# Three 64-wide transposes of a chunked recurrence made as 128x128 transposes, with the sorting of heads left to the copies

## The chip, the cores and the metric

The kernel runs on one core of a Trainium2 chip. The metric is the device time of one execution in microseconds. TensorE multiplies matrices into PSUM, ScalarE and VectorE read PSUM and SBUF, GpSimd works on SBUF alone, and SyncE issues the transfers. Each engine works through its own queue in order and waits for others at semaphores.

## The reference

The program is three small models in a row, each with two layers on 512 positions of width 1024, in float32. The change lies in the last layer of the third model, in a recurrence that runs forwards and backwards over the sequence for 16 heads of width 64. For each head and direction:

```python
def wkv7_step(state, inp):
    r, w, k, v, a, b = inp
    sa = jnp.einsum('...ij,...j->...i', state, a)
    state = (state * w[..., None, :] + sa[..., :, None] * b[..., None, :]
             + v[..., :, None] * k[..., None, :])
    y = jnp.einsum('...ij,...j->...i', state, r)
    return state, y

def rwkv7_bidir_branch(p, mu, w0, w2, a0, a2, k_k, k_a, r_k, lnx_g, lnx_b):
    ...
    init = jnp.zeros((2, bsz, C_HEADS, C_HEAD_DIM, C_HEAD_DIM), jnp.float32)
    xs = (to_scan(r), to_scan(decay), to_scan(k), to_scan(v), to_scan(-kk), to_scan(kk * a))
    _, y = lax.scan(wkv7_step, init, xs)
    y = jnp.moveaxis(y, 0, 2)
    y_sum = y[0] + jnp.flip(y[1], axis=1)
    ...
```

## The kernel before, in words

The function `wkv` does this recurrence in chunks of 64 positions. Its work is cut into 16 steps, one for each pair of heads (c, 0 to 7) and direction (d, 0 or 1). The even steps (d = 0) go forwards, the odd ones (d = 1) backwards. Steps 0 and 1 and steps 14 and 15 are written out; steps 2 to 13 are three rounds of a loop with four steps in it.

An array such as VQ (the values) or BK (the two scaled factors, bhat in `BK[:, 0]` and khat in `BK[:, 1]`) has 128 partitions and 512 columns. Its partitions are channels: 0 to 63 are those of the first head of the pair, 64 to 127 those of the second. Its columns are positions, eight chunks of 64. Some products contract over positions, and for them the step needs the arrays VT, BT and KT, in which the positions of a chunk stand on the partitions: head 0 on partitions 0 to 63, head 1 on 64 to 127, and in the free dimension chunk j with 64 channels.

Each step does two things at once, in an order of instructions written out by hand in `step` for each engine. It prepares its own chunks (projection of the next raw data, norms, decays, the three transposes, three groups of products, five levels of a triangular inverse). And it runs the serial chain over the eight chunks of the step before, of which every link is a few small products on TensorE (`ch_g`, `ch_sa`, `ch_ys`), with a small copy on VectorE (`gk`, L3798), one on ScalarE (`san`, L3720) and the state's update on VectorE (`upd`, L3805) between them. These links stand among the preparation, so that neither waits for long.

The places that matter here, in the order of TensorE's queue in one step:

- `ch_sa(1)`, then the transpose of the values (mark "tv") and that of bhat ("tb"). Each is 16 products of 64x64 through `heads` (L3527): eight chunks times two heads, with the data as the stationary operand and the 64x64 identity as the moving one. They write PSUM banks 4 and 1.
- The product "bon" with the whole array (L3632), and `ch_ys(1)`.
- The transpose of khat ("tk", again 16 products), into bank 4. It waits until ScalarE has copied the values out of this bank ("vt") and VectorE has made khat (L3866).
- `ch_g(2)`, which waits for the state's update `upd(1)`.
- "sa", 16 products, which wait for the copy "bt" on ScalarE and for rhat on VectorE (L3867).
- "srb", 16 products of 64x128 into banks 4 and 5, which wait for the copy "kt" on ScalarE. Behind srb stand `ch_sa(2)`, another 16 such products and the levels.

ScalarE's queue at this place: the copy of a projection, `san(1)` (L3720), then the three copies of whole PSUM banks, "vt", "bt" and "kt" (L3775, one instruction of 128x512 each), then "as" (L3777), which waits for sa. VectorE's: rhat (L3867), "bo" (L3870 or L3872, behind TensorE's bon), `upd(1)` (L3805).

Of the kernel before, what the change touches and what calls it, by code (L numbers as in the profile page):

```python
# [10 lines left out]
ACT = mybir.ActivationFunctionType  # L11
# [4 lines left out]
P = 128  # L16
# [3381 lines left out]
def wkv(K, base, WDA, W2, RZ, out):  # L3398
# [7 lines left out]
    def room(n):  # L3406
        nonlocal at
        at += n
        return K.big(at - n, n)
# [8 lines left out]
    BK = room(2 * T).rearrange("p (m t) -> p m t", m=2)  # L3418
# [3 lines left out]
    RQ, KQ, VQ, LW, AA, L, EP, EN, RN, TMP = (room(T) for _ in range(10))  # L3422
# [6 lines left out]
    hr = lambda h: slice(64 * h, 64 * h + 64)  # L3429
# [3 lines left out]
    def halves(b):  # L3433

        two = K.psflat[:, b * 512:b * 512 + 1024].rearrange("p (b n) -> p b n", b=2)[:, :, 0:256]
        return two.rearrange("p b (j t) -> p b j t", t=64)
    block_of = lambda b, j: halves(b)[:, j // 4, j % 4, :]
    couple = lambda b: K.psflat[:, b * 512:b * 512 + 1024].rearrange("p (j m t) -> p j m t", m=2, t=64)
    chunks_of = lambda half: range(4) if half == "a" else range(4, 8)
    in_half = lambda a, half: a[:, 0:4, :] if half == "a" else a[:, 4:8, :]  # L3440
    bank_half = lambda b, half: halves(b)[:, "ab".index(half), :, :]
    levels = range(1, 6)
# [3 lines left out]
    AM = Marks(K, "wkv_act", "sw aa sqk ln rn ep en eplus ee vt bt kt as " + " ".join(f"t{l}a t{l}b" for l in levels))  # L3446
# [26 lines left out]
    with nc.Block() as block:  # L3473
# [38 lines left out]
        def _(pe):  # L3512
            same, one = K.c("same64"), K.c("cident")
# [10 lines left out]
            def heads(dst, lhsT, rhs, start=True, stop=True):  # L3524

                for h in range(2):
                    mm = pe.matmul(dst[hr(h)], lhsT[hr(h)], rhs[hr(h)], start=start, stop=stop, skip_group_check=True)  # L3527
                return mm
# [53 lines left out]
            def step(n, d, c, par, p, pd, nth, fin=None):  # L3582
# [34 lines left out]
                if n is not None:  # L3617
                    pe.wait_ge(DM.sem, DM.count(n, "max"))
                    K.apart(pe)
                    for j in range(8):  # L3620
                        mm = heads(K.ps[:, 4, 64 * j:64 * j + 64], VQ[:, 64 * j:64 * j + 64], one)
                    mm.then_inc(PM.step("tv"), 1)
                    pe.wait_ge(AM.sem, AM.count(n, "aa"))
                    pe.wait_ge(DM.sem, DM.count(n, "bhat"))
                    K.apart(pe)
                    for j in range(8):
                        mm = heads(K.ps[:, 1, 64 * j:64 * j + 64], BK[:, 0, 64 * j:64 * j + 64], one)
                    mm.then_inc(PM.step("tb"), 1)
                    pe.wait_ge(DM.sem, DM.count(n, "rk"))
                    if fin is not None:  # L3630
                        pe.wait_ge(K.sem("fin_act"), K.count("fin_act", 3 * fin[0] + 2))
                    pe.matmul(K.ps[:, 5, :], same, LW, start=True, stop=True).then_inc(PM.step("bon"), 1)  # L3632
                ch_ys(p, pd, 1)
                if n is not None:
                    pe.wait_ge(AM.sem, AM.count(n, "vt"))
                    pe.wait_ge(DM.sem, DM.count(n, "khat"))
                    K.apart(pe)
                    for j in range(8):
                        mm = heads(K.ps[:, 4, 64 * j:64 * j + 64], BK[:, 1, 64 * j:64 * j + 64], one)
                    mm.then_inc(PM.step("tk"), 1)  # L3640
                ch_g(p, pd, 2)
                if n is not None:
# [3 lines left out]
                    for j in range(8):  # L3646
                        mm = heads(block_of(0, j), AR[:, d, j, 0, :], BK[:, 0, 64 * j:64 * j + 64])
# [4 lines left out]
                    for j in range(8):  # L3652
                        mm = heads(couple(4)[:, j, :, :].rearrange("p m t -> p (m t)"), BK[:, 0, 64 * j:64 * j + 64],
                                   AR[:, d, j, :, :].rearrange("p m t -> p (m t)"))
                    mm.then_inc(PM.step("srb"), 1)
                ch_sa(p, pd, 2)
                if n is not None:
# [3 lines left out]
                    for j in range(8):  # L3661
                        mm = heads(couple(2)[:, j, :, :].rearrange("p m t -> p (m t)"), BK[:, 1, 64 * j:64 * j + 64],
                                   AR[:, d, j, :, :].rearrange("p m t -> p (m t)"))
                    mm.then_inc(PM.step("sk"), 1)
                ch_ys(p, pd, 2)
                for l in levels:
                    if n is not None:
                        pe.wait_ge(GM.sem, GM.count(n, f"c{l}"))
                        for half in "ab":
                            pe.wait_ge(DM.sem, DM.count(n, f"xt{l - 1}{half}" if l > 1 else "x0"))  # L3670
                            K.apart(pe)
                            for j in chunks_of(half):
                                mm = heads(block_of(0, j), C[:, j, :], XT[:, j, :])
                            mm.then_inc(PM.step(f"t{l}{half}"), 1)
                    ch_g(p, pd, l + 2)
                    if n is not None:
# [4 lines left out]
                        for half in "ab":  # L3681
                            pe.wait_ge(AM.sem, AM.count(n, f"t{l}{half}"))
                            K.apart(pe)
                            for j in chunks_of(half):
                                mm = heads(block_of(4, j), X[:, j, :], T1[:, j, :])
                            mm.then_inc(PM.step(f"ct{l}{half}"), 1)
                    ch_sa(p, pd, l + 2)
                    if n is not None and l < 5:
# [3 lines left out]
                        for half in "ab":  # L3692
                            for j in chunks_of(half):
                                mm = heads(block_of(2, j), T1[:, j, :], X[:, j, :])
# [5 lines left out]
            for m in range(4):  # L3700
                pe.wait_ge(K.sem("raw_kept"), K.count("raw_kept", m - 1))
                project(0, m)
            rounds(pe, step, finish)

        @block.scalar
        def _(act):
# [26 lines left out]
            def step(n, d, c, par, p, pd, nth, fin=None):  # L3733
# [38 lines left out]
                if n is not None:  # L3772
                    for name, src, dst, bank in (("vt", "tv", VT, 4), ("bt", "tb", BT, 1), ("kt", "tk", KT, 4)):
                        act.wait_ge(PM.sem, PM.count(n, src))
                        act.activation(dst[:, d].rearrange("p j t -> p (j t)"), K.ps[:, bank, :], ACT.Copy).then_inc(AM.step(name), 1)  # L3775
                    act.wait_ge(PM.sem, PM.count(n, "sa"))
                    act.activation(AS.rearrange("p (b j) t -> p b j t", b=2), halves(0), ACT.Copy).then_inc(AM.step("as"), 1)  # L3777
                san(p, pd, 2)
# [8 lines left out]
            for m in range(4):  # L3787
                keep(0, 0, m)
            rounds(act, step, finish)

        @block.vector
# [137 lines left out]
def rwkv_layer(K):  # L3929

    K.open(0, 4 * T)
    YD = K.big(0, 4 * T)
    K.open(4 * T, 9 * T)
    WD, WDA, W2, RZ = K.big(4 * T, T), K.big(5 * T, 2 * T), K.big(7 * T, 4 * T), K.big(11 * T, 2 * T)
    K.open(13 * T, 16 * T)
    FD = K.big(13 * T, 4 * T)
    DFT = K.big(17 * T, 8 * T).rearrange("p (i n) -> p i n", i=TT)
    DD = K.big(25 * T, 2 * P)
    four = lambda at, n: K.big(at, 4 * n).rearrange("p (g n) -> p g n", g=4)
    WF, WC = four(25 * T + 2 * P, P), four(25 * T + 6 * P, 2 * P)  # L3940
    with Parts(K, 8) as (hi, lo):
        rwkv_front(K, hi, lo, YD, FD, WD, WDA,
                   [(W2, "w2a2"), (RZ, "resets64"), (DFT, "dft"), (DD, "dft_d"), (WF, "fnet_w")])
    K.open(29 * T, 8 * T)
    fourier(K, FD, YD, DFT, DD, WF, WC, four(29 * T, 2 * T))
    K.shut()
    K.shut()
    K.open(13 * T, 43 * T)
    wkv(K, 13 * T, WDA, W2, RZ, K.X.rearrange("p k t -> p (k t)"))
    K.X, K.H = K.H, K.X  # L3950
    K.shut()
    K.shut()
    with Parts(K, 12) as (hi, lo):
        linear_deep(K, hi, lo, 6, add_to(K.X), feed=Feed(K, features(K.H) + tiles_of(YD, 4), hi, lo))
    K.shut()
# [144 lines left out]
```

## Time and profile before

| What | us |
|---|---|
| median of 3 runs | 4751.49 |
| lowest and highest | 4750.6, 4759.0 |
| the profiled execution, its own time | 4748.9 |
| its span | 4746.7 |
| TensorE busy (PE) | 4400.7, 93% of the span |
| VectorE busy (DVE) | 2457.6, 52% |
| ScalarE busy (ACT) | 1608.9, 34% |
| GpSimd busy (POOL) | 320.5, 7% |

The profile comes from one execution. Its span runs from the first to the last instruction; the 2.2 us between span and time lie around it. The `wkv` stage takes about 820 of the 4746.7 us, from 3824 to 4645, together with what directly follows its last step.

In the timelines below, neighbouring instructions of the same kind are merged into one row: its length is that of the whole group, and x is how many records are in it. A float32 product has two records on TensorE, a transpose in TensorE's own transpose form has one; "L3527 x64" is therefore 32 products. A matmul's record is longer than its pitch in the pipeline: the pitch is read from where the next group starts. What stands in brackets is the time in which the engine was idle before, and who released it.

### The profile page before, as it was taken

Reading aid. Unit: us, or ns where it says so; the run is one execution under the profiler, and the core shown is the slowest. Engines: PE = TensorE matmul, PEld = TensorE weight load, DVE = VectorE, ACT = ScalarE, POOL = GpSimd, SP = SyncE. Lnnn points to the kernel's source line nnn. Section 1 sums busy time; section 2 is a strip of 40 time slices with the busy share of each in tenths; the row PEclk is TensorE's granted clock in tenths of the full one; section 3 lists DMA queues with packets and bytes.
Section 4 is the critical chain, followed back from the end, with each engine's and each line's share of the span. In section 5 each row is a group of like instructions: output and inputs, shape, how many; then the busy total and the mean of one; then the engine's idle time right before and its main releaser. Section 6 shows DMA issues by size and latency. Waiting matters only on the chain. (4 is left out here: it accounts for less than half of the span.)

```text
span 4746.7 us, 79005 instructions
## 1 busy us (share of the span) xinstructions
PE 4400.7 (93%) x32172; PEld 3338.7 (70%) x32172; DVE 2457.6 (52%) x3963; ACT 1608.9 (34%) x2467; POOL 320.5 (7%) x307
## 2 busy tenths in 40 slices
PE   8898999899999989999998899978998999999987
PEld 7665788676688767888887644456877567766775
DVE  3634543433445331777777379943534355555553
ACT  2324322323322232666665210133222233334332
POOL 0120000000000000111111000000000022221220
PEclk9888999998999999999999999989998999999998
DMA  3201222221122232111111312111221210000101
GB/s 146 108 19 71 89 89 107 76 89 71 57 104 89 110 129 82 56 59 51 59 54 35 142 53 89 71 54 71 107 98 71 105 37 20 21 20 20 56 3 54
DMA packets 36644, 337.23 MB, mean 71 GB/s; under 512 B 4080, under 2 KB 6384, under 8 KB 18544
## 3 DMA queue, kind: packets, MB, share of 16 engines
q1 hardware_dynamic: 36336, 332.76, 19.0%
q8 instruction: 238, 3.90, 0.3%
q14 instruction: 70, 0.57, 0.0%
HBM read 320.16 MB, written 12.58 MB: 70 GB/s over the span
## 5 line engine op out<-in xcount | busy, mean ns | idle before, releaser
L539 PE MATMUL ps<-hi,weight_parts 128*128 128x512 f32 x5136 | 1611.5, 395 | 120.6 <-DVE lo L406 75.7
L539 PEld LDWEIGHTS ps<-hi,weight_parts 128*128 128x128 f32 x5136 | 979.8, 191 | 340.8 <-issue 122.0
L539 PE MATMUL ps<-lo,weight_parts 128*128 128x512 f32 x2568 | 1011.7, 394 | 0.0
L527 DVE TENSOR_TENSOR weight_parts<-w,weight_parts 128x1024 fp32r<-128x1024 f32 (+1 forms) x336 | 406.8, 1212 | 967.6 <-ACT weight_parts L518 967.5
L518 ACT ACTIVATE weight_parts<-w 128x1024 fp32r<-128x1024 f32 (+1 forms) x336 | 351.7, 1048 | 1197.0 <-PE ps L539 996.1
L539 PEld LDWEIGHTS ps<-lo,weight_parts 128*128 128x128 f32 x2568 | 490.5, 191 | 102.0
L3527 PEld LDWEIGHTS ps<-buffers 64*64 64x64 f32 x12544 | 430.5, 136 | 125.9 <-issue 123.9
L3527 PE MATMUL ps<-buffers 64*64 64x64 f32 x12544 | 460.0, 226 | 52.0 <-issue 27.1
L2409 PE MATMUL ps<-x_parts,column_parts 128*128 128x512 f32 x1536 | 360.7, 392 | 10.5 <-DVE column_parts L2643 9.9
L2884 PE MATMUL ps<-x,w 128*128 128x512 f32 x768 | 331.6, 595 | 6.8 <-PEq L815 6.8
L2409 PEld LDWEIGHTS ps<-x_parts,column_parts 128*128 128x128 f32 x1536 | 286.5, 189 | 69.9 <-DVE column_parts L2643 10.3
L2947 DVE SCALAR_TENSOR_TENSOR buffers<-buffers,vecs 128x392 f32<-128x392 f32 (+14 forms) x480 | 286.8, 678 | 0.0
L2884 PEld LDWEIGHTS ps<-x,w 128*128 128x128 f32 x768 | 146.5, 191 | 191.2 <-issue 191.2
L3520 PE MATMUL ps<-h,w 128*128 128x512 f32 x512 | 228.7, 601 | 1.2 <-PEq L3351 1.2
L3520 PEld LDWEIGHTS ps<-h,w 128*128 128x128 f32 x512 | 96.3, 192 | 117.3 <-issue 115.8
L2434 PE MATMUL ps<-h 128*128 128x128 f32 x1024 | 129.4, 281 | 35.0 <-DVE w L2687 22.3
L2434 PEld LDWEIGHTS ps<-h 128*128 128x128 f32 x1024 | 124.5, 195 | 42.3 <-DVE w L2687 21.9
L3783 ACT ACTIVATE buffers<-ps 128x256 f32<-128x256 f32 x160 | 61.3, 383 | 174.7 <-PE ps L3527 168.9
L3508 POOL TENSOR_TENSOR buffers<-buffers,const 128x512 f32<-128x512 f32 x80 | 101.6, 1270 | 272.2 <-PE ps L3527 200.3
L2643 DVE TENSOR_TENSOR column_parts<-w,column_parts 128x1024 fp32r<-128x1024 f32 x64 | 78.5, 1228 | 58.1 <-ACT column_parts L2515 58.1
L2623 POOL MEMSET w<- 128x1024 f32 x1 | 1.0, 951 | 1542.4 <-POOLq L2130 1542.4
L2409 PE MATMUL ps<-context_parts,column_parts 128*128 128x256 f32 x768 | 104.0, 292 | 0.0
(481 smaller groups left out, 5337.1 us busy)
## 6 DMA issues: line engine op xcount, KB each, us to landing
w<-in_weights SPq DMA_DIRECT2D x126, 2048.0 KB, 7.9
w<-in_wh SPq DMA_DIRECT2D x64, 512.0 KB, 3.6
v_kept<-buffers SPq DMA_DIRECT2D x4, 1024.0 KB, 5.2
buffers<-v_kept SPq DMA_DIRECT2D x16, 256.0 KB, 2.6
h<-x_kept SPq DMA_DIRECT2D x2, 2048.0 KB, 10.5
x<-in_xT SPq DMA_DIRECT2D x4, 512.0 KB, 10.7
x_kept<-h SPq DMA_DIRECT2D x1, 2048.0 KB, 7.0
vc_kept<-x SPq DMA_DIRECT2D x4, 512.0 KB, 2.6
```

The lines of the kernel that those rows point to most:

```text
L518: act.activation(K.parts[:, j % 2, 0, 0:nk, :], part_of(K, slot, j, nk, by_row), ACT.Copy)\
L527: dve.tensor_tensor(K.parts[:, j % 2, 1, 0:nk, :], part_of(K, slot, j, nk, by_row), K.parts[:, j % 2, 0, 0:nk, :].bitcast(F32), ALU.subtra ...
L539: mm = pe.matmul(ps, K.parts[:, j % 2, m, k, :], x[:, k * T:(k + 1) * T], start=(first and k == 0 and n == 0), stop=(last and k == nk - 1 ...
L2409: mm = pe.matmul(o, parts[:, half, w, k, :], src[:, m, k, 0:width], start=(k == 0 and n == 0), stop=(k == 7 and n == 2), skip_group_check= ...
L2434: mm = pe.matmul(bank[:, s], l[:, s], r[:, s], start=True, stop=True)
L2643: dve.tensor_tensor(half[:, 1], weight(name), half[:, 0].bitcast(F32), ALU.subtract).then_inc(DL.step(name), 1)
L2884: mm = pe.matmul(bank(i, j), w[:, k, j * P:(j + 1) * P], K.H[:, k, :], start=(k == 0), stop=(k == 7))
L2947: dve.scalar_tensor_tensor(y, u, w, y, ALU.mult, ALU.add).then_inc(K.sem("tapped"), 1)
L3508: pool.tensor_tensor(C, AS, on_chunks(f"{'clow' if d == 0 else 'cup'}{l}"), ALU.mult).then_inc(GM.step(f"c{l}"), 1)
L3520: mm = pe.matmul(K.ps[:, 2 + m % 2, :], w[:, k, m * P:(m + 1) * P], K.H[:, k, :], start=(k == 0), stop=(k == 7))
L3527: mm = pe.matmul(dst[hr(h)], lhsT[hr(h)], rhs[hr(h)], start=start, stop=stop, skip_group_check=True)
L3783: act.activation(in_half(T1, half), bank_half(0, half), ACT.Copy)\
```

## The change

The three transposes are no longer 16 products each of 64x64, but four `transpose` instructions of 128x128 each, with the data as the moving operand and the 128x128 identity as the stationary one. Such a piece covers two chunks and both heads. In its result the partitions are 128 positions, that is chunk 2q on 0 to 63 and chunk 2q+1 on 64 to 127, and the columns are the channels of head 0 and head 1. So the heads are not yet on the halves of the partitions where VT, BT and KT want them. The copies do that: instead of one instruction of 128x512, ScalarE issues four of 64 partitions by 4x64 columns. `kept` gives their operands: for head h and parity r of the chunk, the source is the half r of the partitions in PSUM, and the destination is the half h in SBUF. The order of the four is (h, r) = (0,0), (0,1), (1,0), (1,1). The banks, the marks, the waits and everything else stay.

```diff
--- before.py
+++ after.py
@@ -3437,6 +3437,11 @@
     block_of = lambda b, j: halves(b)[:, j // 4, j % 4, :]
     couple = lambda b: K.psflat[:, b * 512:b * 512 + 1024].rearrange("p (j m t) -> p j m t", m=2, t=64)
     chunks_of = lambda half: range(4) if half == "a" else range(4, 8)
+
+    def kept(dst, bank, h, r):
+
+        src = K.ps[:, bank, :].rearrange("p (q h t) -> p q h t", h=2, t=64)
+        return dst[hr(h)].rearrange("p (q r) t -> p q r t", r=2)[:, :, r, :], src[hr(r), :, h, :]
     in_half = lambda a, half: a[:, 0:4, :] if half == "a" else a[:, 4:8, :]
     bank_half = lambda b, half: halves(b)[:, "ab".index(half), :, :]
     levels = range(1, 6)
@@ -3617,14 +3622,14 @@
                 if n is not None:
                     pe.wait_ge(DM.sem, DM.count(n, "max"))
                     K.apart(pe)
-                    for j in range(8):
-                        mm = heads(K.ps[:, 4, 64 * j:64 * j + 64], VQ[:, 64 * j:64 * j + 64], one)
+                    for q in range(4):
+                        mm = pe.transpose(K.ps[:, 4, q * P:(q + 1) * P], VQ[:, q * P:(q + 1) * P], K.c("ident"))
                     mm.then_inc(PM.step("tv"), 1)
                     pe.wait_ge(AM.sem, AM.count(n, "aa"))
                     pe.wait_ge(DM.sem, DM.count(n, "bhat"))
                     K.apart(pe)
-                    for j in range(8):
-                        mm = heads(K.ps[:, 1, 64 * j:64 * j + 64], BK[:, 0, 64 * j:64 * j + 64], one)
+                    for q in range(4):
+                        mm = pe.transpose(K.ps[:, 1, q * P:(q + 1) * P], BK[:, 0, q * P:(q + 1) * P], K.c("ident"))
                     mm.then_inc(PM.step("tb"), 1)
                     pe.wait_ge(DM.sem, DM.count(n, "rk"))
                     if fin is not None:
@@ -3635,8 +3640,8 @@
                     pe.wait_ge(AM.sem, AM.count(n, "vt"))
                     pe.wait_ge(DM.sem, DM.count(n, "khat"))
                     K.apart(pe)
-                    for j in range(8):
-                        mm = heads(K.ps[:, 4, 64 * j:64 * j + 64], BK[:, 1, 64 * j:64 * j + 64], one)
+                    for q in range(4):
+                        mm = pe.transpose(K.ps[:, 4, q * P:(q + 1) * P], BK[:, 1, q * P:(q + 1) * P], K.c("ident"))
                     mm.then_inc(PM.step("tk"), 1)
                 ch_g(p, pd, 2)
                 if n is not None:
@@ -3772,7 +3777,10 @@
                 if n is not None:
                     for name, src, dst, bank in (("vt", "tv", VT, 4), ("bt", "tb", BT, 1), ("kt", "tk", KT, 4)):
                         act.wait_ge(PM.sem, PM.count(n, src))
-                        act.activation(dst[:, d].rearrange("p j t -> p (j t)"), K.ps[:, bank, :], ACT.Copy).then_inc(AM.step(name), 1)
+                        for h in range(2):
+                            for r in range(2):
+                                ins = act.activation(*kept(dst[:, d], bank, h, r), ACT.Copy)
+                        ins.then_inc(AM.step(name), 1)
                     act.wait_ge(PM.sem, PM.count(n, "sa"))
                     act.activation(AS.rearrange("p (b j) t -> p b j t", b=2), halves(0), ACT.Copy).then_inc(AM.step("as"), 1)
                 san(p, pd, 2)
```

The first place on TensorE is an even step in the loop, from the transpose of the values (behind `ch_sa(1)`) to bon:

```order
L3527 MATMUL ps<-const,buffers 64x64 [waits wkv_dve]
L3527 MATMUL ps<-const,buffers 64x64 x15
L3623 REGISTER_ALU
L3624 REGISTER_ALU [waits wkv_act]
L3527 MATMUL ps<-const,buffers 64x64 [waits wkv_dve]
L3527 MATMUL ps<-const,buffers 64x64 x15
L3629 REGISTER_ALU
L3632 MATMUL ps<-buffers,const 128x512 [waits wkv_dve]
```

The same rows of the changed kernel, whose line numbers are five higher:

```order
L3626 MATMUL ps<-const,buffers 128x128 [waits wkv_dve]
L3626 MATMUL ps<-const,buffers 128x128 x3
L3628 REGISTER_ALU
L3629 REGISTER_ALU [waits wkv_act]
L3632 MATMUL ps<-const,buffers 128x128 [waits wkv_dve]
L3632 MATMUL ps<-const,buffers 128x128 x3
L3634 REGISTER_ALU
L3637 MATMUL ps<-buffers,const 128x512 [waits wkv_dve]
```

Each set of 16 products has become a set of four transposes. Nothing has changed places, and the waits in front of the sets are the same.

The second place on TensorE is the transpose of khat, with `ch_g(2)` and sa behind it:

```order
L3635 REGISTER_ALU
L3636 REGISTER_ALU [waits wkv_act]
L3527 MATMUL ps<-const,buffers 64x64 [waits wkv_dve]
L3527 MATMUL ps<-const,buffers 64x64 x15
L3543 REGISTER_ALU
L3527 MATMUL ps<-buffers 64x64 [waits ch_s]
L3527 MATMUL ps<-buffers 64x64 x7
L3643 REGISTER_ALU
L3644 REGISTER_ALU [waits wkv_act]
L3527 MATMUL ps<-buffers 64x64 [waits wkv_dve]
L3527 MATMUL ps<-buffers 64x64 x15
```

And in the changed kernel:

```order
L3640 REGISTER_ALU
L3641 REGISTER_ALU [waits wkv_act]
L3644 MATMUL ps<-const,buffers 128x128 [waits wkv_dve]
L3644 MATMUL ps<-const,buffers 128x128 x3
L3548 REGISTER_ALU
L3532 MATMUL ps<-buffers 64x64 [waits ch_s]
L3532 MATMUL ps<-buffers 64x64 x7
L3648 REGISTER_ALU
L3649 REGISTER_ALU [waits wkv_act]
L3532 MATMUL ps<-buffers 64x64 [waits wkv_dve]
L3532 MATMUL ps<-buffers 64x64 x15
```

Here too only the set itself differs.

The place on ScalarE is the same step, from `san(1)` to the copy kt:

```order
L3720 ACTIVATE buffers<-ps 128x64 [waits ch_sa]
L3774 REGISTER_ALU
L3775 ACTIVATE buffers<-ps 128x512 [waits wkv_pe]
L3774 REGISTER_ALU
L3775 ACTIVATE buffers<-ps 128x512 [waits wkv_pe]
L3774 REGISTER_ALU
L3775 ACTIVATE buffers<-ps 128x512 [waits wkv_pe]
L3776 REGISTER_ALU
```

And in the changed kernel, where L3782 is the line of the four copies:

```order
L3725 ACTIVATE buffers<-ps 128x64 [waits ch_sa]
L3779 REGISTER_ALU
L3782 ACTIVATE buffers<-ps 64x4x64 [waits wkv_pe]
L3782 ACTIVATE buffers<-ps 64x4x64 x3
L3779 REGISTER_ALU
L3782 ACTIVATE buffers<-ps 64x4x64 [waits wkv_pe]
L3782 ACTIVATE buffers<-ps 64x4x64 x3
L3779 REGISTER_ALU
L3782 ACTIVATE buffers<-ps 64x4x64 [waits wkv_pe]
L3782 ACTIVATE buffers<-ps 64x4x64 x3
L3784 REGISTER_ALU
```

Each copy of a whole bank has become one copy that waits and three that follow it without a wait.

## Rows read from the trace of the kernel before

**Rows 1.** Stretch of the chunk stage: from:to, length, busy us and instructions per engine, clock.

```profile
3824.00:4645.00 821.00, 752.79 (x15034) 575.67 (x15032) 434.58 (x928) 295.49 (x586) 173.28 (x172) 0.97 0.06 23
```

**Rows 2.** What TensorE waited for in that stretch: total us, times, longest.

```profile
PE ps L3527 <- issue: 31.6, 41, 4.3
```

**Rows 3.** DMA queue of instructions in that stretch: packets, MB, share.

```profile
q8 instruction: 126, 2.06, 1.0%
```

**Rows 4.** Timeline, step 3 (odd): start, length, engine, line, out<-in, count, [idle before].

```profile
3969.42 2.03 PE L3527 MATMUL ps<-const,buffers 64*64 64x64 f32 x64
...
3970.22 0.22 ACT L3720 ACTIVATE buffers<-ps 128x64 f32<-128x64 f32 x1
3970.56 0.60 ACT L3775 ACTIVATE buffers<-ps 128x512 f32<-128x512 f32 x1
...
3971.37 0.68 DVE L3867 TENSOR_TENSOR buffers<-buffers 128x512 f32<-128x512 f32 x1
...
3971.38 1.12 PE L3632 MATMUL ps<-buffers,const 128*128 128x512 f32 x2
...
3972.44 0.33 PE L3527 MATMUL ps<-buffers 64*64 64x64 f32 x4
...
3972.54 0.69 DVE L3872 TENSOR_TENSOR buffers<-ps,buffers 128x512 f32<-128x512 f32 x1 [0.49 <-PE ps L3632]
...
3972.95 1.10 PE L3527 MATMUL ps<-const,buffers 64*64 64x64 f32 x32
3973.15 0.27 DVE L3805 TENSOR_SCALAR buffers<-ps,buffers 128x64 f32<-128x64 f32 x1
...
3973.88 3.32 PE L3527 MATMUL ps<-buffers 64*64 64x64 f32 x80
3974.10 0.60 ACT L3775 ACTIVATE buffers<-ps 128x512 f32<-128x512 f32 x1 [2.00 <-PE ps L3527]
```

**Rows 5.** Timeline, step 4 (even), the same place.

```profile
4022.21 2.03 PE L3527 MATMUL ps<-const,buffers 64*64 64x64 f32 x64
4022.64 0.22 ACT L3720 ACTIVATE buffers<-ps 128x64 f32<-128x64 f32 x1
4023.35 0.60 ACT L3775 ACTIVATE buffers<-ps 128x512 f32<-128x512 f32 x1 [0.49 <-PE ps L3527]
...
4026.67 5.29 PE L3527 MATMUL ps<-buffers 64*64 64x64 f32 x120
```

**Rows 6.** Timeline, an earlier stage: TensorE transposes of 128x128, and what follows.

```profile
1916.97 0.60 PE L2453 MATMUL ps<-const,h 128*128 128x128 f32 x4
1917.40 1.95 PE L2434 MATMUL ps<-h 128*128 128x128 f32 x16
```

**Rows 7.** Timeline, the same stage: ScalarE copies on part of the partitions.

```profile
1918.50 0.55 ACT L2564 ACTIVATE w<-ps 32x128 f32<-32x128 f32 x2 [0.30 <-PE ps L2434]
1919.39 0.38 ACT L2564 ACTIVATE w<-ps 64x256 f32<-64x256 f32 x1 [0.35 <-PE ps L2434]
1919.67 1.04 ACT L2531 ACTIVATE x<-head_inputs 128x1024 f32<-128x1024 f32 x1
...
1940.52 0.38 ACT L2564 ACTIVATE w<-ps 64x256 f32<-64x256 f32 x1 [0.34 <-PE ps L2434]
1940.92 1.48 ACT L2531 ACTIVATE x<-head_inputs 128x1536 f32<-128x1536 f32 x1
```

**Rows 8.** Groups of that line, by shape: busy us, mean ns.

```profile
L2564 ACT ACTIVATE w<-ps 32x128 f32<-32x128 f32 x64 | 17.1, 268 | 37.7 <-PE ps L2434 37.3
```

**Rows 9.** Timeline: TensorE released by a copy of ScalarE.

```profile
3948.48 0.22 ACT L3720 ACTIVATE buffers<-ps 128x64 f32<-128x64 f32 x1 [1.13 <-PE ps L3527]
...
3948.85 0.33 PE L3527 MATMUL ps<-buffers 64*64 64x64 f32 x4 [0.41 <-ACT buffers L3720]
```

**Rows 10.** Timeline, step 1, the same place as in rows 4.

```profile
3868.49 1.09 ACT L3775 ACTIVATE buffers<-ps 128x512 f32<-128x512 f32 x2
...
3871.08 5.18 PE L3527 MATMUL ps<-buffers 64*64 64x64 f32 x116
```

## The prediction

> **What bounds the kernel now.** I first read the totals of the chunk stage: in its 821 us TensorE is busy for 753 us at a mean granted clock of 0.97, in 15034 matmul and 15032 weight-load records [rows 1]. So TensorE's queue sets the pace, and a cut of its work counts unless something else comes late. The waits of TensorE say how little else there is: its largest item there, "issue", is 31.6 us in 41 pauses that no other engine explains [rows 2].
>
> Then I read one odd and one even step in the timeline, at the three transposes. In step 3 [rows 4] TensorE runs tv and tb in 3969.42 to 3971.38 (64 records in 1.96 us, so 0.98 us a set), bon to 3972.44, ch_ys(1) in 0.51 us to 3972.95, tk to about 3973.88 (0.93 to 0.98 us). The row of 80 records behind it is ch_g(2) (16), sa (32) and srb (32 of double width). At the pitch of tv and tb, 0.0305 us a record, rounded to 0.47 us for 16 and 0.94 us for 32, srb begins at 3973.88 + 1.41 = 3975.29. TensorE does not stop on this way. ScalarE is at leisure: its copies start at 3970.56 and, after 2.00 us idle, at 3974.10. In step 4 [rows 5] tv starts at 4022.21, the first copy 1.14 us later as in step 3, ch_g(2) at 4026.67 and srb at 4028.08. From vt's start to srb it is thus 4.73 us in both. Of the 16 steps, the twelve in the loop look like these two, six of each kind.
>
> **TensorE's part.** The trace has the new form in another stage: four transposes of 128x128 occupy TensorE for 1917.40 - 1916.97 = 0.43 us, one record each [rows 6]. A set falls from 0.98 to 0.43 us, three sets by 1.65 us a step. Going from 64-wide work to whole-array work and back costs something: bon is two records of 128x512, and takes 1.06 us to the next group, where its own length of 1.12 us is already the sum of two overlapping ones [rows 4]. tk now has such an edge on either side, and tv gets the one that bon had. I take 0.1 us at each new edge, 0.2 us a step. If nothing else came late, this were 16 x 1.45 = 23 us.
>
> **ScalarE's part.** Three copies of 128x512 at 0.60 us become twelve of 64x256. The trace has this shape: 0.38 us [rows 7]. What decides is the pitch of such copies in a row. After the 64x256 copy at 1919.39 the next instruction starts at 1919.67, 0.28 us later and before the first one's end; after the one at 1940.52 it starts at 1940.92, 0.40 us later, with no overlap [rows 7]. The code tells the two apart: the first reads and writes from partition 0, as its follower does; the second sits on partitions 64 to 127, and its follower starts at 0. A pair of 32x128 copies at different partitions takes 0.55 us together with 0.27 us each, again no overlap [rows 7, 8]. In the changed kernel the source half changes at every one of the twelve copies, and the destination half at every second. So the likely pitch is that of copies which don't overlap: 0.39 us, between 0.38 and 0.40.
>
> The Trainium skill (ScalarE: Activation LUTs, section "What ACT_TABLE_LOAD costs") says that back-to-back ACTIVATEs overlap by about 93 ns. The pitch of 0.28 agrees with that, those of 0.40 and of the pair of 32x128 do not. By the rule alone the pitch would be 0.28 us, which is the first rival below.
>
> With 0.39 us the chain of the copies is 11 x 0.39 + 0.38 = 4.67 us, and 0.15 us until TensorE goes on (a copy ends at 3948.70, TensorE starts at 3948.85 [rows 9]): 4.82 us from vt's start to srb, where it was 4.73.
>
> vt starts earlier, though. The odd step: tv is ready before ScalarE's san(1) of 3970.22 is through, so vt follows that at 3970.34 in place of 3970.56. srb then starts at 3970.34 + 4.82 = 3975.16, 0.13 us sooner. I checked what else could be later than this. The tail of VectorE: rhat ends at 3972.05, then bo (0.61 us until the update starts, from 3972.54 to 3973.15), the update's 0.27 us and 0.15 us to TensorE give ch_g(2) at 3973.08 [rows 4], sa at 3973.6 (its copy bt ends at 3973.45), its end at 3974.6: earlier than 3975.16. So ScalarE becomes the bound. The even step: vt starts after 0.43 + 0.1 + 0.16 = 0.69 us in place of 1.14 us (the 0.16 us is what lay between tv's end and the copy: 1.14 - 0.98), at 4022.90, just after san(1) (4022.64 + 0.22 [rows 5]). srb starts at 4027.72 in place of 4028.08, 0.36 us sooner. Together 6 x (0.13 + 0.36) = 2.9 us gained.
>
> The written-out steps have less slack. In step 1 vt cannot start before 3868.49 and srb started at 3871.08 + 1.41 = 3872.49 [rows 10]; now 3873.31, 0.8 us later. For step 0, where the copies too were closer to the end of TensorE's own work, I put 0.6 us lost, for step 15 0.1 us, for step 14 nothing (VectorE is late there): 1.5 us lost, an estimate.
>
> **Fewer instructions.** A set loses 56 of 64 records (32 matmuls and 32 weight loads become 4 and 4), a step 168, the stage 2688 of 30066, or 9%. The queue that brings instructions moved 126 packets [rows 3], one for every 239 records, so 11 fall away. If all 31.6 us of unexplained pauses came from them, that were 31.6 / 126 x 11 = 2.8 us. I take half to two thirds of it, 1.7 us; the ends are nothing and 2.8.
>
> **Sum.** -2.9 + 1.5 - 1.7 = -3.1 us. The profiled execution took 4748.9 us (span 4746.7 and 2.2 around it) and would take 4745.8; on the median of 4751.5, which lies 2.6 above it, 4748.4. I say 4748. What is behind srb (sk, the levels, the next step) hangs on srb, so it moves with it. The copy "as" finds ScalarE free as soon as kt is out.
>
> **The rivals.**
>
> 1. The copies overlap. If only a change of the destination mattered, the mean pitch were about 0.34 us, and 11 x 0.05 = 0.55 us a step or 8 us more would be gained: 4740. If nothing mattered (0.28 us), the copies' chain is 3.6 us. The odd step is then held by VectorE (ch_g(2) at 3973.0, sa, srb at 3974.4: 0.9 us gained), the even one by TensorE itself (1.3 us gained); with the edges 6 x 2.2 + 1 + 1.7 = 16 us: 4735.5. For it: the row at 1919.39. Against it: the two other places.
>
> 2. The copies are dearer, so the kernel is slower. No row shows a copy whose source half is not its destination half, as two of each four are, so the upper end is the longest nearby copy: 0.60 us for a whole bank of 128x512, with a pitch of about 0.6. The point from which ScalarE costs more than TensorE gives is near: (3975.29 - 0.15 - 0.38 - 3970.34) / 11 = 0.402 us in the odd step, 0.423 in the even one. At 0.50 us, halfway, each step loses 11 x 0.11 = 1.2 us against my sum, 18 us in 15 steps: 4766. At 0.6 it is 4783. Against it: 64x256 took what its columns ask.
>
> 3. The clock. The granted clock was 0.97 over the stage [rows 1]. If transposes and the new pause before srb let it fall from 2.4 to 1.2 GHz until srb is through, sa and srb take 0.94 + 1.8 us more, 0.6 of it in the pause: 2 us in 15 steps, 4778. The Trainium skill (TensorE: Matmul & The Clock Gate, Part 4) says that a transpose does not count as activity for the clock gate. Six stand among other matmuls in the stage of rows 6 without a drop that I see in their pitch (0.107 us each); four at a time are little beside what is around them.
>
> 4. All of TensorE's gain arrives, because the copies' results are not what srb waits for: 4748 - 20 = 4726. The order of the queue speaks against it: srb writes the bank that kt is copied from.
>
> **How the numbers follow.** The forecast 0.48, its own range 4742 to 4755 (a pitch of 0.37 to 0.41 and the packets' term). Rival 1 0.29, rival 2 0.16, rival 3 0.04, rival 4 0.03. I count as "same" what lies within 0.2%, 9.5 us, which is about what a measurement of this kernel can tell from no change. Faster: 0.29 of rival 1, some of which ends inside the band, 0.03 and a little of the forecast's tail: 0.32. Slower: 0.20 and as little: 0.21. The rest is the same, 0.47. The range leaves out the far end of the dear copies, the clock and rival 4: 4733 to 4766.
>
> **What would show it.** Right: twelve copies of 64x256 at about 0.39 us pitch with hardly a gap from vt to kt, and in front of srb a new wait of TensorE for ScalarE of about half a microsecond, while the sets on TensorE take 0.43 us. Wrong: a pitch of 0.28 us and a wait for VectorE's update in the odd steps (rival 1), single copies above 0.42 us (rival 2), a granted clock below 0.97 in the stage (rival 3), or no wait before srb (rival 4). The term of the packets is wrong if TensorE's unexplained pauses in the stage do not fall from 31.6 us.

## The result and the profile after

| | before | after |
|---|---|---|
| median of 8 runs each, us | 4753.4 (4747.8 to 4760.0) | 4769.5 (4766.5 to 4774.9) |
| ratio, 95% interval | | 1.0032 [1.0023, 1.0041] |
| span of the profiled execution, us | 4746.7 | 4767.4 |

The change makes the kernel 0.3% slower, 16 us by the medians and 20.7 us between the profiled executions (that of before ran 4.5 us below the median of its kernel, so part of the 20.7 is that). The forecast was 4748, and 4733 to 4766 its range: wrong. Of its sum the part that was worked out in most detail came out as forecast, and the time came from a place that had hardly been looked at.

The page of after: the whole span, the busiest engines, and the group of plain 64x64 matmuls (busy us, mean ns of one, idle before it).

```profile
span 4767.4 us, 76461 instructions
...
PE 4391.6 (92%) x30828; PEld 3319.6 (70%) x30828; DVE 2458.8 (52%) x3963; ACT 1653.4 (35%) x2611; POOL 320.5 (7%) x307
...
L3532 PE MATMUL ps<-buffers 64*64 64x64 f32 x12544 | 468.8, 226 | 76.9 <-issue 40.0
```

The chunk stage of after, as rows 1 had it: from:to, length, busy us and count of PE, PEld, DVE, ACT, POOL, granted clock, DMA share and GB/s. Then, of the same stretch, the waits of TensorE (us, times, longest), and the DMA queue of instructions.

```profile
3824.00:4665.70 841.70, 742.71 (x13690) 557.18 (x13688) 435.06 (x928) 339.72 (x730) 173.32 (x172) 0.96 0.06 22
```

```profile
PE ps L3532 <- issue: 42.4, 49, 1.6
PE ps L3532 <- DVE buffers L3813: 16.8, 43, 1.1
PE ps L3532 <- ACT buffers L3725: 9.4, 23, 0.4
PE ps L3532 <- ACT buffers L3782: 9.1, 23, 0.9
PE ps L3601 <- issue: 7.7, 3, 3.9
...
PE ps L3632 <- issue: 5.5, 2, 4.7
```

```profile
q8 instruction: 115, 1.88, 0.9%
```

TensorE has 1344 records fewer and is 10 us less busy [rows 1], the queue of instructions moved 11 packets fewer [rows 3], and yet TensorE's waits for "issue", for which no other engine accounts, rose from 31.6 [rows 2] to 42.4 us. The group of before contains the transposes, with one pause of 4.3 us ahead of a transpose in step 15; in after the transposes stand apart, and their 5.5 us of L3632 belong to the comparison. Like for like the rise is from 31.6 to 47.9 us.

Step 3 of after, to be held against rows 4: start, length, engine, line, operation, count.

```profile
3973.93 0.66 PE L3626 MATMUL ps<-const,buffers 128*128 128x128 f32 x4
3974.36 0.22 ACT L3725 ACTIVATE buffers<-ps 128x64 f32<-128x64 f32 x1
3974.42 0.60 PE L3632 MATMUL ps<-const,buffers 128*128 128x128 f32 x4
3974.62 4.70 ACT L3782 ACTIVATE buffers<-ps 64x256 f32<-64x256 f32 x12
3974.86 1.07 PE L3637 MATMUL ps<-buffers,const 128*128 128x512 f32 x2
...
3976.47 0.66 PE L3644 MATMUL ps<-const,buffers 128*128 128x128 f32 x4
...
3977.42 1.71 PE L3532 MATMUL ps<-buffers 64*64 64x64 f32 x48 [0.30 <-DVE buffers L3813]
3979.56 3.94 PE L3532 MATMUL ps<-buffers 64*64 64x128 f32 x72 [0.42 <-ACT buffers L3782]
```

This is what was forecast: a set takes 0.49 us on TensorE to tb and 0.44 to bon, the twelve copies stand back to back, 4.70 us in a row (forecast 4.67), and srb, the first of the last group, waits 0.42 us for ScalarE. It starts 4.94 us after vt (forecast 4.82).

Where the 20.7 us lie, from the starts of the steps and of srb in the two timelines:

| part | before | after | change | forecast |
|---|---|---|---|---|
| start of the span to step 2 | 3898.0 | 3901.4 | +3.4 | +1.4 |
| steps 2 to 13, up to srb | 309.3 | 307.3 | -2.0 | -2.9 |
| steps 2 to 13, from srb to the next step | 320.8 | 334.8 | +14.0 | 0, and -1.7 for fewer packets |
| steps 14 and 15 and the rest | 218.6 | 223.8 | +5.2 | +0.1 |

(12.1 us for the loop in sum, with rounding.) From srb on the two kernels have the same instructions: sk, the five levels, the products of the next step. A step took there, over the places 2/6/10, 3/7/11, 4/8/12 and 5/9/13 of the loop, 26.4, 27.8, 24.7 and 28.1 us before, and 27.9, 28.4, 27.6 and 27.7 after. The third differs most. Step 8, one of these three, first in before from inside srb on (24.85 us from srb, at 4238.58, to the next step), then in after (27.65 us):

```profile
4246.80 3.93 PE L3527 MATMUL ps<-buffers 64*64 64x64 f32 x128
4250.65 4.04 PE L3527 MATMUL ps<-buffers 64*64 64x64 f32 x127
...
4256.99 2.13 PE L3527 MATMUL ps<-buffers 64*64 64x64 f32 x65 [0.31 <-issue]
...
4261.18 1.58 PE L3527 MATMUL ps<-buffers 64*64 64x64 f32 x39 [0.42 <-issue]
...
4263.43 0.69 PE L3596 MATMUL ps<-buffers 64*128 64x512 f32 x1
```

```profile
4246.61 3.94 PE L3532 MATMUL ps<-buffers 64*64 64x128 f32 x72 [0.42 <-ACT buffers L3782]
4250.36 0.31 PE L3532 MATMUL ps<-buffers,const 64*64 64x64 f32 x4
4250.47 1.36 PE L3532 MATMUL ps<-buffers 64*64 64x64 f32 x40
4252.17 2.78 PE L3532 MATMUL ps<-buffers 64*64 64x64 f32 x88 [0.34 <-DVE buffers L3813]
4254.76 0.31 PE L3532 MATMUL ps<-buffers,const 64*64 64x64 f32 x4
4254.88 3.69 PE L3532 MATMUL ps<-buffers 64*64 64x64 f32 x120
4259.56 0.46 PE L3532 MATMUL ps<-buffers 64*64 64x64 f32 x8 [0.99 <-issue]
4259.84 0.29 PE L3532 MATMUL ps<-buffers,const 64*64 64x64 f32 x4
4259.96 3.33 PE L3532 MATMUL ps<-buffers 64*64 64x64 f32 x108
4264.91 0.74 PE L3532 MATMUL ps<-buffers 64*64 64x64 f32 x19 [1.63 <-issue]
4269.41 1.09 PE L3532 MATMUL ps<-buffers 64*64 64x64 f32 x30 [0.78 <-issue]
4274.26 0.69 PE L3601 MATMUL ps<-buffers 64*128 64x512 f32 x1
```

After stops for 0.99, 1.63 and 0.78 us, before for 0.31 and 0.42 us. The counts tell where: from the first row of after to the first stop 72 + 4 + 40 + 88 + 4 + 120 = 328 records, to the next 8 + 4 + 108 = 120 more. A packet of the queue is 1.88 MB / 115 = 16.3 KB (16,384 bytes each, by the DMA records), and one of them was issued at 4256.98 and landed at 4258.13, 1.4 us before TensorE went on at 4259.56. So my theory (placing, "P" in the expectations) was: TensorE's own instructions come in packets, one for some 120 matmul records (60 products) with their weight loads and waits, and between two packets it can stand still. A level is about as long, 118 to 121 records, so in a step the ends of packets fall at the same place of every level: at a bad one each costs 1 to 2 us, at a good one under 0.5. The change took 168 instructions from each step and so moved these places. Rivals: that the change itself costs (the copies, "C", by their new form, or the transposes), or that ScalarE's longer work delays what is behind srb.

The DMA records bear the theory out further than these two stops. In steps 2 to 13 of all fourteen kernels of this document TensorE has 497 "issue" pauses in the group of 64x64 matmuls, and every one of them ends 1.2 to 1.7 us after such a packet has landed (median 1.4). While the levels run, packets come some 4 to 5 us apart, so this is no chance. They also say what makes one end dear and another cheap: how far ahead the packet is issued. Ahead of the 180 pauses of 1 us and more it was issued when TensorE was 39 records from the end of its old packet (median; 4 to 55), ahead of the 126 pauses under 0.5 us 68 records (34 to 83). In step 8 of before the end that lies 413 records behind srb costs nothing: its packet was issued at 4250.35, 83 records ahead. In step 8 of after the packets of the first two stops were issued 47 and 35 records ahead. What sets the moment of issue is not shown.

### The profile page after: what moved, and what is told of

Read it like the earlier page. It is cut to its first block and busy times, and to the rows that moved or that the text cites. A ratio compares the mean times of both kernels' runs of the same rounds, so it can differ in the third digit from the quotient of the medians.

```text
span 4767.4 us, 76461 instructions
## 1 busy us (share of the span) xinstructions
PE 4391.6 (92%) x30828; PEld 3319.6 (70%) x30828; DVE 2458.8 (52%) x3963; ACT 1653.4 (35%) x2611; POOL 320.5 (7%) x307
## 3 DMA queue, kind: packets, MB, share of 16 engines
q1 hardware_dynamic: 36336, 332.76, 18.8%
```

## The experiments

All ratios are to the kernel before, timed beside each version; its median was 4754 to 4756 us there.

| | median, us | ratio, 95% | steps 2 to 13, us | of it behind srb | "issue", us (times) |
|---|---|---|---|---|---|
| before | 4753 | 1 | 630.1 | 320.8 | 21.0 (31) |
| after | 4769.5 | 1.0032 [1.0023, 1.0041] | 642.1 | 334.8 | 34.5 (38) |
| 1 copies only | 4760.7 | 1.0012 [1.0003, 1.0021] | 643.1 | 327.6 | 25.3 (40) |
| 2 transposes only | 4759.7 | 1.0010 [1.0001, 1.0019] | 634.9 | 338.3 | 36.3 (43) |
| 3 after, 128 increments | 4761.5 | 1.0014 [1.0005, 1.0024] | 630.1 | 323.2 | 22.7 (31) |
| 4 before, 128 increments | 4779.3 | 1.0050 [1.0037, 1.0064] | 653.5 | 343.5 | 43.3 (40) |
| 5 before, 256 matmul instructions | 4757.3 | 1.0008 [0.9999, 1.0017] | 634.3 | 323.2 | 21.6 (32) |
| 6 after, 128 of them | 4750.8 | 0.9995 [0.9986, 1.0004] | 627.1 | 319.2 | 18.8 (26) |
| 7 after, copies split | 4759.8 | 1.0016 [1.0007, 1.0025] | 636.8 | 329.8 | 30.4 (35) |
| 8 split, 128 of them | 4747.8 | 0.9984 [0.9975, 0.9993] | 627.4 | 319.1 | 20.2 (27) |
| 9 before, 64 of them | 4777.1 | 1.0041 [1.0028, 1.0055] | 660.7 | 345.7 | 44.0 (44) |
| 10 before, 128 of them | 4767.5 | 1.0024 [1.0015, 1.0033] | 648.9 | 339.3 | 39.9 (39) |
| 11 before, 192 of them | 4761.8 | 1.0011 [1.0002, 1.0020] | 641.3 | 330.3 | 28.8 (41) |
| 12 split, 64 of them | 4755.1 | 0.9998 [0.9989, 1.0007] | 637.3 | 329.1 | 27.3 (30) |

The last column is TensorE's waits for "issue" in the group of 64x64 matmuls, steps 2 to 13. The three columns on the loop come from one execution each, while a median is over five or more: differences of a few us between two loops can be those of two executions.

**1 and 2: each part alone.**

```diff
 # 1, in before: the three whole copies in four pieces each, data where they were
-  act.activation(dst[:, d].rearrange("p j t -> p (j t)"), K.ps[:, bank, :], ACT.Copy)
+  for h in range(2):
+    for r in range(2):
+      ins = act.activation(dst[...][hr(h)]..., src4[hr(h), :, r, :], ACT.Copy)
 # 2, in after: the transposes kept, each set copied out whole
-  for h in range(2):
-    for r in range(2):
-      ins = act.activation(*kept(dst[:, d], bank, h, r), ACT.Copy)
+  act.activation(dst[:, d]..., K.ps[:, bank, :], ACT.Copy, scale=1.0 / 64)
```

> The kernel before with its 64-wide products kept, and only each of the three whole-bank copies cut into four of 64x256. TensorE's records do not change in number, so the instruction packets fall where they fell. Theory P (the loss of the changed kernel comes from where instruction packets fall in TensorE's stream): srb starts 0.1 us later in each of the 12 loop steps (12 copies and the way to TensorE take 4.82 us in place of 4.73), 0.8 to 1.0 us later in steps 0 and 1: 2 to 4 us slower than before, ratio 1.0005 to 1.001. Theory C (the copies themselves cost it, through ScalarE or something behind it): 12 to 18 us slower, 1.003 to 1.004.

> The changed kernel with its transposes, but each copy whole again in one instruction of 128x512, scaled by 1/64; the heads are not put on their halves, so the data behind is other data. TensorE's records are those of the changed kernel. Theory P: srb comes about 0.9 us sooner than before in odd and 1.3 us in even steps (13 to 15 us), and the packets fall as badly as in the changed kernel (15 us lost behind srb): within 5 us of before. Theory C: nothing is lost, so 14 to 17 us faster than before, ratio 0.9965 to 0.997.

Experiment 2 leaves out the sorting of the heads, so the data behind are others; the instructions of TensorE are those of after. The transposes alone gain 0.86 us in an odd and 1.35 us in an even step up to srb (12.7 us in the loop), and lose 17.5 us behind srb, where nothing was edited. So the loss is not the copies'. In all it is 5.3 us slower than before, where theory P had said within 5 and theory C 14 to 17 faster. The copies alone come to +6 us, between the two expectations. They cost 0.4 us in most steps up to srb, more than I had said (and 2.0 us in step 6, which begins with 6.8 in place of 3.4 us at the low clock): with the old tk the kt copies start only when tk is through and last 1.55 in place of 0.60 us. Of the loop's 13.0 us they are 6.2; 6.8 lie behind srb. But the two profiled executions are 14.9 us apart and the medians only 6.3, so these 6.8 us are no more than what the choice of executions can make, and a loss behind srb is not shown for the copies. The pauses stand at the same records as in before (379, 499 and 621 behind srb in step 2, for one), as they must if copies on ScalarE take no instruction from TensorE's queue.

**3 and 4: 128 increments of a semaphore in TensorE's queue, once, in step 0.** They compute nothing and are off every later step; all they do to the loop is to move where packets end, by half a packet.

```diff
                 ch_sa(p, pd, 1)
+                if p is None:
+                    for _ in range(128):
+                        K.apart(pe)
```

> The changed kernel, with 128 increments of a semaphore that nobody waits for put in TensorE's queue once, in step 0 behind a projection of 7 us. They shift all that follows by half an instruction packet; no work is added or removed in steps 1 to 15. Theory P: the pauses behind srb, which sat at matmul record 252, 327 or 227 of the stretch and every 121 records after it, move 64 records forward to places at which the kernel before showed short ones in three of the four loop steps: 6 to 14 us less than the changed kernel, ratio to before about 1.000 to 1.002. Theory C and a theory of the clock: no difference from the changed kernel, at most 3 us more.

> The kernel before with the same 128 increments at the same place and nothing else. Theory P: its pauses move 64 records forward too, to where the changed kernel shows the long ones in three of the four loop steps: 8 to 20 us slower than before, ratio 1.002 to 1.004, with not one engine instruction changed. Theory C: no more than 3 us slower.

In after the loop falls from 642.1 to 630.1 us, in before it rises from 630.1 to 653.5. The loops and their "issue" waits, first after and 3, then before and 4:

```profile
3901.40:4543.55 642.15, 576.49 (x10345) 422.90 (x10345) 334.77 (x709) 267.34 (x565) 132.43 (x132) 0.99 0.07 26
```

```profile
3910.25:4540.30 630.05, 576.20 (x10344) 423.87 (x10345) 334.92 (x709) 266.99 (x565) 132.39 (x132) 0.99 0.07 26
```

```profile
PE ps L3532 <- issue: 22.7, 31, 1.4
```

```profile
3898.00:4528.09 630.09, 586.84 (x11353) 437.97 (x11353) 334.69 (x709) 234.30 (x457) 132.36 (x132) 0.99 0.07 26
```

```profile
3910.61:4564.08 653.47, 587.32 (x11353) 438.54 (x11353) 335.19 (x709) 234.67 (x457) 132.60 (x132) 0.99 0.07 25
```

```profile
PE ps L3527 <- issue: 43.3, 40, 1.9
```

The instructions of the loop are those of after and of before, one for one, and their busy time is the same within 0.5 us. What differs is how long TensorE stands at "issue". The pauses have moved by some 60 records, half a packet: in step 4 of after they stand 328, 448 and 569 records behind srb, in 3 at 509 and 630; in step 2 of before at 379, 499 and 621, in 4 at 318, 438 and 560. Experiment 4 came to 25 us over before, where 8 to 20 had been expected. The increments were not free, though: TensorE was held up in step 0 by 11.9 us, about 0.09 us for each.

```profile
3821.81 1.02 PE L3520 MATMUL ps<-h,w 128*128 128x512 f32 x2
3834.70 3.68 PE L3527 MATMUL ps<-const,buffers 64*64 64x64 f32 x64 [11.87 <-issue]
```

**5, 9, 10, 11: matmuls in their place, a quarter to a whole packet.** The values' 16 products were done again in step 0, one to four times, before the real ones. A product of fp32 has two matmul and two weight-load records, so each time adds 64 instructions, and four times make a packet.

```diff
                     K.apart(pe)
+                    for _ in range(R if p is None else 0):
+                        for j in range(8):
+                            heads(K.ps[:, 4, 64 * j:64 * j + 64], VQ[:, 64 * j:64 * j + 64], one)
```

> The kernel before, with the 16 products of the values' transpose done four times more in step 0 only: 64 products, 256 records of TensorE, about 3.9 us. With 64 B an instruction, as 16.3 KB a packet over 239 records suggest, 256 instructions are one whole packet, so all that follows keeps its place within a packet. Theory P: steps 1 to 15 take what they took before, each within 0.5 us or so, and the whole 3 to 6 us more than before, ratio 1.0005 to 1.0015, far from the extra 12 us beyond the padding's own cost that half a packet gave. Theory Q (any shift of the code disturbs the stage, or such padding does): 12 us or more beyond the 3.9.

> The kernel before, with the 16 products of the values' transpose done once more in step 0: 64 instructions, a quarter of a packet, 1 us. Theory P, read from the pauses of all kernels so far: counted in matmul records from srb, modulo a packet's 121, a boundary between 160 and 193 (45 to 78 behind record 115) gives short pauses, one between 200 and 255 long ones. The four loop steps of before stand at 21, 36, 56, 71 behind record 115 and come to 110, 4, 24, 39: one in the good place, two doubtful, one bad. 5 to 14 us slower than before.

> The same done twice: 128 instructions, half a packet as in e4, for 2 us in place of 13 us. Theory P: the loop steps as in e4, so e4's 4779 less 11 us: 12 to 16 us slower than before. A theory in which the 128 increments themselves did the harm: 2 to 4 us slower.

> The same done three times: 192 instructions, 3 us. The four loop steps come to 46, 61, 81 and 96 behind record 115: two good, two at the bad side. Theory P: 2 to 9 us slower than before.

The median against before goes 0, +21, +12, +6 and, at a whole packet, +3 us, of which 3.7 us are the added work itself. More work costs less, and at a whole packet the steps are nearly those of before again (behind srb 323.2 us, before 320.8). The pauses stand again at the records of before (379, 499 and 621 in step 2). So the period is 256 instructions, which in 16,384 bytes are 64 bytes each. Of the sizes only 11 came as expected (2 to 9 us): 10 fell just short of its 12 to 16, and 9, expected at 5 to 14 us and below 10, cost 21 and was the dearest. Half a packet of matmuls (10: 648.9 us for the loop) does to before what half a packet of increments did (4: 653.5), without the 11.9 us ahead, and its pauses stand at the records of 4.

**6: the cheap shift in after.** The same edit with R = 2.

> The changed kernel, with 16 products of the kernel before done twice in step 0 as padding: 128 instructions, half a packet as in e3, but for 2 us in place of the 11 us that the 128 increments took. Theory P: the loop steps as in e3, 17 to 20 us less behind srb than in the changed kernel, so 15 to 18 us less in all: ratio to before 0.9985 to 1.0005. A theory in which the increments themselves had helped: as slow as the changed kernel, 1.003.

```profile
3900.32:4527.38 627.06, 576.37 (x10344) 424.03 (x10345) 334.74 (x709) 267.33 (x565) 132.62 (x132) 0.99 0.07 26
```

```profile
PE ps L3532 <- issue: 18.8, 26, 1.5
```

2 us of useless matmuls take 19 us from the kernel, 4769.5 to 4750.8. Behind srb it is 15.6 us less than in after, where 17 to 20 had been expected. The loop is now 3.0 us shorter than before's. That this is near the forecast 2.9 is luck: only 1.4 us of it lie before srb (307.9 against 309.3), and behind srb the packets end at other places than in before. The places 5/9/13 take 31.7 us there against 28.1 and 4/8/12 26.2 against 24.7, the other two some 3 us less than in before.

**7, 8, 12: ScalarE relieved.** Of tb's and tk's pieces the two that read partitions 64 to 127 go to VectorE; sa waits for them.

```diff
-                    pe.wait_ge(DM.sem, DM.count(n, "rhat"))
+                    pe.wait_ge(DM.sem, DM.count(n, "bt2"))
...
-                            for r in range(2):
+                            for r in range(2 if name == "vt" else 1):
...
+                    for name, src, dst, bank in (("bt2", "tb", BT, 1), ("kt2", "tk", KT, 4)):
+                        dve.wait_ge(PM.sem, PM.count(n, src))
+                        for h in range(2):
+                            ins = dve.tensor_copy(*kept(dst[:, d], bank, h, 1))
+                        ins.then_inc(DM.step(name), 1)
```

> The changed kernel, with two of the four copies of bhat and of khat (those that read partitions 64 to 127) moved from ScalarE to VectorE, behind the state's update. ScalarE has 8 copies where it had 12, and TensorE's instructions are those of the changed kernel, with sa waiting for VectorE's copies in place of rhat. The chain before srb gets shorter: srb 0.5 us sooner than in the changed kernel in odd steps, 0.7 to 0.9 in even ones, 8 to 10 us in all. The packets fall as in the changed kernel, and so do the pauses behind srb, by theory P: ratio to before 1.000 to 1.002. By theory C, in which ScalarE's work is what the changed kernel lost by, it would be faster than before by 5 us or more.

> e7 and the padding of e6 together. By theory P both gains add: 8 to 10 us less than e6, ratio to before 0.9965 to 0.999. By theory C the padding adds its 2 us to e7.

> e8 with one repeat as padding in place of two, 64 instructions. The four loop steps come to 106, 80, 60 and 32 behind record 115, one bad, the others good or fair: within 4 us of e8, 4744 to 4752, ratio to before 0.998 to 0.9995.

An even step (8) and an odd one (3) of 7:

```profile
4239.82 0.77 ACT L3782 ACTIVATE buffers<-ps 64x256 f32<-64x256 f32 x2
4240.46 1.76 DVE L3886 COPY buffers<-ps 64x256 f32<-64x256 f32 x4
4240.74 0.77 ACT L3782 ACTIVATE buffers<-ps 64x256 f32<-64x256 f32 x2 [0.16 <-PE ps L3644]
4241.47 5.07 PE L3532 MATMUL ps<-buffers 64*64 64x64 f32 x104 [0.15 <-DVE buffers L3886]
```

```profile
3974.32 1.77 DVE L3886 COPY buffers<-ps 64x256 f32<-64x256 f32 x4
3976.11 0.69 DVE L3892 TENSOR_TENSOR buffers<-buffers 128x512 f32<-128x512 f32 x1
3976.95 3.94 PE L3532 MATMUL ps<-buffers 64*64 64x128 f32 x72 [0.47 <-DVE buffers L3892]
```

VectorE takes 0.44 us a piece, and in the odd step bo2 stands behind the four and srb behind bo2: srb is 0.38 us later there than in after, in the even step 0.58 us sooner. The relief is worth a tenth of a microsecond a step, and 7 is faster than after mostly since TensorE pauses less. With half a packet more (8) it is 4747.8 us, the only version that was measured faster than both, by 0.16% of before; 3 us better than 6, where 8 to 10 had been expected; the intervals of 6 and 8 overlap, so that they differ is not shown. A quarter packet (12) gave 4755.1, outside the 4744 to 4752 expected: I could say ahead neither what one placing gives nor, with 9, which is the worst.

## Why the prediction was wrong, point by point

- **TensorE's part**: right. Up to bon most steps are 0.94 (odd) and 1.05 us (even) shorter (step 6 by 0.1 and step 10 by 1.7, which begin at the low clock), and the transposes alone bring srb 0.86 and 1.35 us sooner (experiment 2); forecast 0.9 and 1.3.
- **ScalarE's part**: right. The pitch was 0.387 to 0.394 us inside a set and 0.403 to 0.405 from set to set, forecast 0.39, whether the source half changes alone or both do. This is what excluded rivals 1 and 2. The sentence of the Trainium skill (ScalarE: Activation LUTs, "What ACT_TABLE_LOAD costs") on the overlap of back-to-back ACTIVATEs holds at none of these changes of half.
- **Step to step up to srb**: net 0.15 (odd) and 0.26 us (even) sooner, forecast 0.13 and 0.36. In sum 1.9 of 2.9 us. The twelve copies took what was forecast; from the end of the last one to srb it was 0.24 us in step 3, where 0.15 had been put.
- **The edges**: steps 0 and 1 lost 0.4 and 0.9 us before srb, as forecast; the rest of the 3.4 us lies behind srb of step 1.
- **Fewer instructions**: the failed step. I took the pauses as a sum that falls with the number of packets, -1.7 us between 0 and -2.8, and wrote that what is behind srb "hangs on srb, so it moves with it". The 11 packets did fall away, and the pauses rose from 31.6 to 47.9 us, the transposes' own among them. A packet's end costs by its place, from nothing that is seen to nearly 2 us, and the loop lost 14.0 us behind srb. The end of my range for this term should have been on the other side of zero too: 31.6 us in 41 pauses of the same group [rows 2] for 126 packets [rows 3] says that most packets' ends cost nothing there and the others 0.7 us in the mean (without the one pause of 4.3 us), and a change of 168 instructions a step reshuffles which.
- **Rival 3, the clock**: not in the loop, where the granted clock is 0.99 in both (10.2 us in all at the low level, at the start of steps 6 and 10), but at its end. Of the last 5.2 us, 2.4 lie before srb of step 14, while TensorE runs at 1.2 GHz (0.50). First before, then after:

```profile
4531.30:4538.10 6.80, 5.85 (x64) 4.05 (x66) 5.64 (x10) 5.21 (x10) 0.00 (x0) 0.50 0.00 0
```

```profile
4548.50:4562.20 13.70, 11.09 (x109) 7.95 (x109) 9.09 (x18) 7.99 (x20) 1.46 (x2) 0.50 0.00 1
```

  It stays at the low level for 13.7 in place of 6.8 us, in which TensorE starts its transposes with pauses of 0.8 to 1.1 us ahead of them:

```profile
4550.45 1.58 PE L3532 MATMUL ps<-buffers 64*64 64x64 f32 x20 [1.05 <-DVE buffers L3813]
4551.96 1.11 PE L3626 MATMUL ps<-const,buffers 128*128 128x128 f32 x4
...
4553.85 1.08 PE L3632 MATMUL ps<-const,buffers 128*128 128x128 f32 x4 [0.78 <-issue]
...
4555.72 2.08 PE L3637 MATMUL ps<-buffers,const 128*128 128x512 f32 x2 [0.78 <-DVE buffers L3870]
```

  This goes with the transposes. In all seven kernels that have them (after, 2, 3, 6, 7, 8, 12) the low stretch of step 14 lasts 10.2 or 13.7 us, in all seven with 64-wide products (before, 1, 4, 5, 9, 10, 11) 6.8, and from the step's start to srb it is 17.5 to 18.8 us against 16.3 to 16.5. In experiment 2, with whole copies, the stretch is 10.2 us (4540.08 to 4550.32) and the step 1.1 us longer up to srb. So rival 3 happened, once and not in 15 steps. Whether the transposes do it or the pauses between them was not separated. Another 3.5 us lie behind srb of step 15, where after has more and longer "issue" pauses.

What is shown: moving the packets' ends, with the loop unchanged, takes the kernel before from 4756 to 4777 us and after from 4769.5 to 4750.8. That is more than either part of the change. Every pause follows the landing of a packet, and it is dear where the packet was issued late. What stays open: what sets the moment at which a packet is issued (whether the last wait ahead of it decides), and so why it is late at one place of a level and not at another. The change itself was timed at two placings only, so what it gives on average over the placings is not known.

## What to carry to other kernels

Where TensorE's queue is dense with small matmuls, look for "issue" pauses that come at one distance counted in records: they are packet ends, and any edit that adds or drops instructions ahead of a loop shifts them all. Forecast such an edit with a term of both signs, as large as the pauses in the trace. Before judging it, time it and its base at two or three shifts of a fraction of a packet; here a single comparison gave +16 us for a change that gains 2 us in the loop up to srb, and whose place in the packets decides the rest.

## What the runs showed that I had not expected

- A packet of TensorE's instructions is 16,384 bytes, 256 instructions, some 120 records of 64x64 matmuls with their weight loads; its end costs between nothing and 1.9 us, and TensorE goes on 1.2 to 1.7 us after the packet has landed.
- Between two rounds of the loop TensorE stands still for 3.4 to 5.4 us, in every kernel here.
- 128 increments of a semaphore in TensorE's queue take 11.9 us, 0.09 us each, while 128 instructions of real matmuls take 2 us.
- VectorE copies 64x256 out of PSUM in 0.44 us, ScalarE in 0.38 us at a pitch of 0.39.
